# A weight ring of five raw and two rounded pieces, sample rows loaded through GpSimd's queue, and an expert choice in three parts

## The reference

```python
h = _rms_norm(x, g_pre_mix) * (1.0 + sc_a) + sh_a
q, k, v, xl, yl, ga, gr = jnp.split(h @ w_in, ...)
o_attn = sliding_window_attention(q, k, v)              # window 128, 16 heads
o_lru = rg_lru(causal_conv(xl)) * gelu(yl)
merged = sigmoid(ga) * (o_attn @ w_attn_branch) + sigmoid(gr) * (o_lru @ w_lru_branch)
mix = merged @ w_out
x = x + gt_a * _rms_norm(mix, g_post_mix)
h2 = _rms_norm(x, g_pre_ffn) * (1.0 + sc_f) + sh_f
# router: best of 4 groups, best 2 of its 8 experts, softmax weights
f = _hier_moe(h2, ...)                                  # 32 SwiGLU experts, 1024 -> 512 -> 1024
x = x + gt_f * _rms_norm(f, g_post_ffn)
```

## Time and the profile before

| what | value |
|---|---|
| median of 3 runs | 2003.75 us (2003.07 to 2009.68) |
| the profiled execution's own time | 2002.22 us |
| its span, first to last instruction | 2000.4 us |
| mean granted clock of TensorE | 0.952 of full |
| busy: TensorE, VectorE, ScalarE, GpSimd | 1773.6, 1294.2, 1037.5, 257.5 us |

### The profile page before, as it was taken

One profiled execution on the slowest core, in us unless ns is written; L12 is line 12 of the kernel. 1 busy time (PEld: TensorE's weight loads), 2 busy tenths in 40 slices (PEclk: granted clock), 3 DMA queues, 4 the chain that ended last, 5 costly groups with the idle time before them and its releaser, 6 DMA issues.

```text
span 2000.4 us, 24197 instructions
## 1 busy us (share of the span) xinstructions
PE 1773.6 (89%) x8882; PEld 1396.1 (70%) x8882; DVE 1294.2 (65%) x1626; ACT 1037.5 (52%) x1414; POOL 257.5 (13%) x284
## 2 busy tenths in 40 slices
PE   3899978999999999999999995499999999999970
PEld 0566645666666689999999984377777777877760
DVE  4302236777777773454554645688888888888857
ACT  2413334444545553343543532467777777777744
POOL 0000001222222000000000000022121121131314
PEclk9899988999999999999999996699999999999995
DMA  9463220111111355553565546578898988888946
GB/s 350 169 239 116 74 90 4 35 46 46 46 46 46 111 158 173 178 170 125 170 198 181 193 143 236 190 292 337 358 376 352 370 341 345 360 340 355 363 178 260
DMA packets 93799, 408.03 MB, mean 204 GB/s; under 512 B 14854, under 2 KB 39590, under 8 KB 77320
## 3 DMA queue, kind: packets, MB, share of 16 engines
q1 hardware_dynamic: 78480, 384.45, 51.6%
q0 software_dynamic: 10080, 17.33, 2.3%
q10 hardware_dynamic: 5160, 5.18, 0.8%
HBM read 380.51 MB, written 46.81 MB: 214 GB/s over the span
## 4 chain that ended last, share of the span: by engine, by line
PE 61%; DMA 15%; DVE 12%; issue 5%; ACT 4%; POOL 2%; SPq 1%; ACTq 0%; POOLq 0%; DVEq 0%
PE ps L1670 58%; DMA xg<-h_dram,idx 10%; DMA wg<-w_gate 2%; PE ps L1968 1%; PE ps L1810 1%; DVE olst L1314 1%; POOL idx L747 1%; DMA wraw<-w_ga 1%; DVE mx L1263 1%; DMA wA<-w_xl 1%; DMA nsink<-sinks 1%; ACT wg_up L1072 1%; DVE xc L1286 1%; DVE xc L1305 1%; PE ps L1889 1%
## 5 line engine op out<-in xcount | busy, mean ns | idle before, releaser
L935 ACT ACTIVATE wup<-wraw 128x1024 fp32r<-128x1024 f32 x120 | 126.6, 1058 | 254.9 <-PE ps L1670 179.4
L1369 DVE TENSOR_TENSOR wlow<-wraw,wup 128x1024 fp32r<-128x1024 f32 x120 | 146.4, 1223 | 167.9 <-ACT wup L935 167.5
L1670 PE MATMUL ps<-hT,wA 128*128 128x352 f32 x624 | 195.9, 471 | 13.7 <-ACT hT L792 12.0
L1670 PE MATMUL ps<-hT,wB 128*128 128x352 f32 x624 | 189.2, 459 | 0.5 <-ACT gB L879 0.5
L1670 PEld LDWEIGHTS ps<-hT,wA 128*128 128x128 f32 x624 | 120.4, 195 | 83.0 <-ACT hT L792 12.3
L1592 DVE TENSOR_TENSOR wd_low<-wd,wd_up 128x2048 fp32r<-128x2048 f32 x68 | 152.9, 2289 | 23.6 <-ACT wd_up L1082 23.6
L1592 DVE TENSOR_TENSOR wu_low<-wu,wu_up 128x2048 fp32r<-128x2048 f32 x68 | 155.5, 2288 | 17.3 <-ACT wu_up L1077 17.3
L1592 DVE TENSOR_TENSOR wg_low<-wg,wg_up 128x2048 fp32r<-128x2048 f32 x68 | 152.7, 2287 | 19.4 <-ACT wg_up L1072 19.0
L1670 PEld LDWEIGHTS ps<-hT,wB 128*128 128x128 f32 x624 | 118.4, 190 | 64.1 <-issue 1.9
L1077 ACT ACTIVATE wu_up<-wu 128x2048 fp32r<-128x2048 f32 x68 | 130.0, 1913 | 32.8 <-PE ps L1670 32.8
L1072 ACT ACTIVATE wg_up<-wg 128x2048 fp32r<-128x2048 f32 x68 | 126.5, 1910 | 16.4 <-DMA wg<-w_gate 15.9
(11 more groups left out here) (317 smaller groups left out, 4093.6 us busy)
## 6 DMA issues: line engine op xcount, KB each, us to landing
wg<-w_gate SPq DMA_DIRECT2D x34, 2048.0 KB, 12.9
wu<-w_up SPq DMA_DIRECT2D x34, 2048.0 KB, 12.6
wd<-w_down SPq DMA_DIRECT2D x34, 2048.0 KB, 8.3
wada<-w_ada SPq DMA_DIRECT2D x12, 2048.0 KB, 11.0
wraw<-w_ga SPq DMA_DIRECT2D x24, 512.0 KB, 3.6
wraw<-w_gr SPq DMA_DIRECT2D x24, 512.0 KB, 3.5
wraw<-w_at SPq DMA_DIRECT2D x24, 512.0 KB, 3.6
wraw<-w_lr SPq DMA_DIRECT2D x24, 512.0 KB, 3.6
```

Of the source, the lines that this page charges most:

```text
L935: act.activation(wup[n % UP][:, :, :], wraw[n % RAW][:, :, :], ACT.Copy).then_inc(w_rounded, 1)
L1369: V.tensor_tensor(wlow[n % RAW][:, :, :], wraw[n % RAW][:, :, :], wup[n % UP][:, :, :].bitcast(F32), ALU.subtract).then_inc(w_split, 1)
L1670: return pe.matmul(out, lhsT, rhs, start=start, stop=stop, skip_group_check=True)
```

## The change

The merge ring has five raw pieces and two rounded ones, seven buffers as before at the same addresses. The order of the loads is the same; `more_weights` only leaves out those that were issued ahead of the loop. The 24 sample row loads go from SP's queue to GpSimd's, behind the same wait for `out` 1,7, with a semaphore of their own, `ld_samples`. The expert choice of the first six tiles is made in three calls of two tiles, behind `keep_mix` of q = 0, 1 and 4. The eight loads of G2s stay on SP.

```diff
-RAW, UP = 4, 3
+RAW, UP = 5, 2
...
+            def more_weights(key):
+                if STEP[key] >= RAW:
+                    load_weights(key)
...
-                    if STEP["ga", g, o] >= RAW:
-                        load_weights(("ga", g, o))
+                    more_weights(("ga", g, o))
...
-                    if (g, o) != (0, 0):
-                        load_weights(("gr", g, o))
+                    more_weights(("gr", g, o))
...
-                    if (g, o) != (0, 0):
-                        load_weights(("at", g, o))
+                    more_weights(("at", g, o))
...
-                    if (g, o) == (2, 6):
-                        sp.wait_ge(step_done, STEP["out", 1, KC - 1] + 1)
-                        for a, h, ts in ((0, 0, G1s), (1, 0, A2s), (0, 2, B2s)):
-                            spread_samples(a, h, ts)
...
+            pool.wait_ge(step_done, STEP["out", 1, KC - 1] + 1)
+            for a, h, ts in ((0, 0, G1s), (1, 0, A2s), (0, 2, B2s)):
+                for b in range(NB):
+                    pool.dma_start(ts[NT * b:NT * (b + 1), :].rearrange("p (h n) -> p h n", h=2),
+                                   mod_dram[a, h:h + 2, 1 + b:2 + b, :].rearrange("h r n -> r h n").broadcast_to([NT, 2, 512])).then_inc(ld_samples, 16)
...
-                        dve.wait_ge(ld_spread, 16 * 3 if g < GRP - 1 else 16 * 3 * (1 + NB))
+                        dve.wait_ge(ld_spread, 16 * 3)
+                        if g == GRP - 1:
+                            dve.wait_ge(ld_samples, 16 * 3 * NB)
...
-            for q in range(4):
+            for q in range(KC):
                 keep_mix(last, q)
-            best(0, 3 * last)
-            for q in range(4, KC):
-                keep_mix(last, q)
+                if q in (0, 1, 4):
+                    t0 = 2 * min(q, 2)
+                    best(t0, t0 + 2)
...
-            dve.wait_ge(ld_spread, 16 * 4 * (1 + NB))
+            dve.wait_ge(ld_spread, 16 * (4 + NB))
```

More of the change, by code:

```diff
@@ L349, in build @@
         ld_w = [sem(f"ld_w{i}") for i in range(RAW)]
-        ld_spread, ld_route, ld_xin, ld_masks = sem("ld_spread"), sem("ld_route"), sem("ld_xin"), sem("ld_masks")
+        ld_spread, ld_samples, ld_route, ld_xin, ld_masks = sem("ld_spread"), sem("ld_samples"), sem("ld_route"), sem("ld_xin"), sem("ld_masks")
         ld_src = [sem("ld_h"), sem("ld_o"), sem("ld_ol")]
@@ L561, in spread_rows @@
                              mod_dram[g, h:h + 2, r0:r0 + 1, :].rearrange("h r n -> r h n").broadcast_to([P, 2, 512])).then_inc(ld_spread, 16)
[L563 to L567, removed]
             def load_x(g):
@@ L661, in _ @@
             spread_rows(1, 2, G2p, 0)
-            spread_samples(1, 2, G2s)
+            for b in range(NB):
+                sp.dma_start(G2s[NT * b:NT * (b + 1), :].rearrange("p (h n) -> p h n", h=2),
+                             mod_dram[1, 2:4, 1 + b:2 + b, :].rearrange("h r n -> r h n").broadcast_to([NT, 2, 512])).then_inc(ld_spread, 16)
             sp.wait_ge(tables, 1)
```

## The result

The changed kernel takes 2014.98 us (median of 8 runs, 2008.16 to 2020.83) against 2004.26 us (8 runs) of the kernel before: ratio 1.0049, 95% interval 1.0029 to 1.0068, so 9.8 us slower (5.8 to 13.6). Forecast were 7.5 us slower than before and 2011 us. The profiled execution spans 2007.0 us, 6.6 more than before.

A forecast was written before the change was run, and what follows sets the result against it. TensorE's work plus its gaps was taken to bound the merge stage. Nine terms summed to +7.15, +7.5 with the clock, from 2002.2 to 2009.7 profiled; as median 2011 us against 2003.75, range 2003 to 2018.

The forecast's parts named there:

- The chain of 2.4 us in a step of 4.2 or 3.15: Steady pace: preparing a piece fits within the one step that runs meanwhile, with 1.8 or 0.75 us to spare; no cost.
- (a): Start of the merge stage: third split comes late, TensorE idles 6.9 us and the clock falls; +5.3 us (2.9 to 7.1).
- (b): Split behind the x1 multiplies: waits of 0.85 us twice in group 1, +1.7, and 2.0 once in group 2, +2.0.
- (c): At the norms: piece late, +1.7 us in group 1; group 2's gap replaces the wait for h2, +2.1 (0 to 5.9).
- (d): Turnovers to groups 1 and 2: split of the first `ga` piece late behind the source split; +1.3 us (0.4 to 3.6).
- (e): Fourth `ga` piece: its load is let go one step sooner by the raw depth, gap gone; -3.0 us (0 to -3.0).
- (f): 24 sample loads off SP's queue: the gap on kept logits behind the late `ga` 2,7 goes; -3.0 us (-2 to -3.0).
- Sample rows on GpSimd's queue cost nothing: The 24 loads moved there take 60 us, to 1169, before VectorE wants them about 1198.4; no cost.
- (g): Expert choice in parts: 1.85 us before the last split goes, new wait of 0.85 to 0.9; -0.95 us (0 to -1.85).
- that of the clock: Rival: TensorE's clock falls at new gaps of about 2 us or more, four more falls give 7: 2018 us, chance 0.13.
- the two signs of being wrong: Waits on `wlow` summing to under 8 us, or the span behind the last `out` step differing by more than 2 us.
- Two pieces suffice: Rival: splits are less late than counted, double-buffering hides the losses and a gain of 6.95 remains: 1997 us, chance 0.08.

The follow-up runs named there:

- experiment 10: The changed kernel run once more, nothing altered: ratio 1.0041 to the kernel before, merge stage 531.8 us.
- Experiment 4: Changed kernel with the third piece's rounding ahead of the gate's square and its split right behind the scan: ratio 1.0023 to the kernel before, stage 527.6 us.
- experiment 3: Changed kernel with the split of the next piece moved ahead of the x1 multiplies in `keep_mix`: ratio 1.0000 to the kernel before, stage 522.7 us.
- experiment 5: Changed kernel with four raw pieces instead of five, still two rounded: ratio 1.0085 to the kernel before, stage 540.5 us.
- experiment 2: Changed kernel with only the ring of five and two kept; sample loads back on SP's queue, choice in one call: ratio 1.0076 to the kernel before.
- experiment 1: Changed kernel with the ring back at four raw and three rounded pieces: ratio 0.9979 to the kernel before, stage 517.4 us.
- experiment 6: Changed kernel with split ahead of x1 multiplies, third piece's split early, x1's square sums behind the rounding that follows `at`: ratio 0.9968 to the kernel before.
- experiment 7: Changed kernel with four raw and three rounded pieces, and six row loads issued one per round: 1994.93 us, ratio 0.9949 to the kernel before.

## Why the prediction was right

The direction, the range and the nine terms' signs held, and the places of all nine. Point by point:

- **The chain of 2.4 us in a step of 4.2 or 3.15 costs nothing in the steady pace.** Right: between the places of the table the steps of both kernels keep their distance to 0.1 us.
- **(a)** The idle forecast at 6.9 was 6.96. The clock charge of 2.4 was 1.8 in the changed kernel, whose step took 6.0 in place of 4.2, and 2.8 in experiment 10; both lie within its bounds. Experiment 4 shows the mechanism: one split moved gave back 3.5 at this place.
- **(b)** The mechanism is shown by experiment 3. Waits of 0.85 and 2.0 were forecast, and 0.95 and 2.04 measured. A restart costs some 0.25 more than the idle (954.51 - 0.96, but the steps behind it 1.2 later), which I had left out; 0.16 of it is only that idle is counted from the end of the last product, and a step in an unbroken row starts 0.16 ahead of that. In group 2 the clock fell behind the first wait: 3.8 where I had 2.0.
- **(c)** The size was off, +6.7 where I had +3.8. In group 1 the sum charged nothing for the clock, and the 2.10 was followed by half clock; experiment 10 has the gap (2.08) without it, and there the term is 1.7, as forecast. So the fall was 1.35. In group 2 the step that failed is "with the same clock loss": half clock lasted from 1138.7 to about 1144.6 after, 5.9 us, and before the change from 1128.9 to about 1132.3, 3.4 us. A window of 2 us holds 10 products at half clock and 18 at full, so the 2.5 us more are about 1.1 of the 1.55. Windows of the changed kernel, then of the kernel before:

```profile
1138.00:1140.00 2.00, 1.27 (x5) 0.50 0.53 186
...
1142.00:1144.00 2.00, 2.00 (x10) 0.50 0.00 0
1144.00:1146.00 2.00, 2.00 (x15) 0.84 0.32 29
```

```profile
1130.00:1132.00 2.00, 2.00 (x10) 0.50 0.00 0
1132.00:1134.00 2.00, 2.00 (x16) 0.92 0.00 0
1134.00:1136.00 2.00, 2.00 (x18) 1.00 0.41 68
```

- **(d)** 1.9 against 1.3, within its bounds. The split that the prediction reads at 850.91 was that of `gr` 1,0 before the change; it stands at the place in VectorE's order that `ga` 1,0 has now, and only in this sense is the reading right. That an earlier raw load shortens this wait is shown by experiment 5: 2.03 with four raw pieces, 1.07 with five.
- **(e)** Right in the changed kernel, by the raw depth; experiment 5 has it back.
- **(f)** The gain is real but booked to the wrong edit alone: with five raw pieces the load is in time even behind the 24 (experiment 2). The sum is not changed by it, since the gain was counted once.
- **Sample rows on GpSimd's queue cost nothing.** Right in the changed kernel, not in general: with four and three they cost about 1.0 through a weight load beside them (experiment 1). GpSimd in order of time: 24 issues in 14 us, where I had allowed 60.

```profile
1120.02 4.90 POOL L724 DMA_DIRECT2D G1s<-mod_dram  x8 [445.14 <-PE ps L1671]
1124.91 4.65 POOL L724 DMA_DIRECT2D A2s<-mod_dram  x8
1129.57 4.65 POOL L724 DMA_DIRECT2D B2s<-mod_dram  x8
```

  VectorE first used them at 1210.8, long after the last had landed. The loads of G1s took 2.4 to 3.3 us to land, those of B2s 5.0 to 6.4, while the DMA engines were 0.98 busy. VectorE's window there:

```profile
1130.00:1135.00 5.00, 1.45 (x2) 1.00 0.98 363
```

  The warning of the Trainium skill ("SBUF — State Buffer", "SBUF: two separate sides") is about a VectorE operation in a 2-port mode, for which it names the fp32 copy. VectorE ran no such copy from 1120 to 1137, so this trace doesn't test it.
- **(g)** Right. Forecast were a new wait of 0.85 to 0.9 (0.87 came) and the 1.85 gone.

Of the rivals, that of the clock came in part: it fell behind four of the five waits of 2 us and more, of which the sum had charged that of the start and a part of that before `ga` 2,5. The stage lost 4.9 us more than the 7.15 summed. By the table, (b), (c) and (d) came 2.5, 2.9 and 0.6 dearer, and (a), (e), (f) and (g) together 1.1 cheaper. The clock makes 1.55 at (b) and 1.35 and 1.1 at (c), and eight restarts of 0.25 make 2.0; less the 1.1 that is the 4.9, to some tenths. That the ratio of the runs, 9.8 us, lies nearer to the forecast than the stages do is no merit of the sum.

Of the two signs of being wrong the first did not come: the waits on `wlow` sum to 20.5 us. The second did. What lies behind the last `out` step differs by 3.3 us where I had allowed 2. In the twelve profiles what lies behind the stage takes 766.8 to 774.2 us, so the limit was narrower than the scatter between executions, and it decides nothing.

"Two pieces suffice", the rule of the Trainium skill ("Trainium Kernel Development and Optimization", Best Practices: double-buffer), was wrong for this order. With another order it is nearly right: experiment 6 is 2.3 us of stage shorter than the kernel before, but 4.7 longer than three pieces at their best (experiment 7). What stays open is why the third move of experiment 6 did not empty the norms of group 2; I did not take it apart.

## What to carry to other kernels

The depth of a ring is cover for whatever an in-order queue holds ahead of the next piece. Before taking a buffer from a ring, count at each irregular place (start, turnover, norms) the time from the event that lets the piece go to its end on the last engine, and compare it with the steps that are left; the steady pace says nothing. Where it fails, try first to move the piece ahead of the other work, one line here for 9.8 us. And a late load behind a burst can be cured by spreading the burst, which costs no buffer.

## What the runs showed of the hardware

- **Gaps of the same length on TensorE did or did not bring half clock.** Five profiles have the same gaps (the changed kernel, 2, 4, 5 and 10). The 2.04 us before `gr` 2,2 did in three of them (the changed kernel, 4, 10), the 2.04 before `gr` 2,4 in none; 2.08 to 2.10 before `ga` 1,5 did in three (the changed kernel, 4, 5) and not in 2 and 10. At the fourth `ga` 3.03 did not, 2.79 and 2.74 did. A fall at such a gap cost 1.3 to 1.6 us. Of 0.95 none did. Experiment 10 and the changed kernel, windows behind the gap before `ga` 1,5:

```profile
974.00:976.00 2.00, 2.00 (x13) 1.00 0.00 0
```

```profile
972.00:974.00 2.00, 2.00 (x8) 0.50 0.00 0
```

- **A plain DMA of 16 KB issued by GpSimd** took 0.59 us of its time and landed in 2.1 to 6.4 us. The same load took 0.34 us of SP's time, and 0.50 on average for the first eight of experiment 2.
- **A 512 KB load of SP's beside such loads** landed in 4.6 us (experiment 1) and 5.0 us (experiment 7), against 3.6 us for the same load before the change.
- **The first product came at 705.3 to 711.5 us** in twelve profiles whose code is the same up to there but for the ring's first pieces. In the chain that ended last, loads of `wA` stand on it one to four times, at 6.4 to 8.7 us each. What lies behind the stage took 766.8 to 774.2 us. Each scatter is about half the size of what was to be measured, which is why the stage was read start to end.
